# Gate columns of the last 512 tokens multiplied in another stage

## What is computed

```python
h = rms_norm(x, norm_w) * (1 + scale) + shift
proj = h @ w_in                                   # 2888 columns
u_pool, g_pool, q, k, v, g_attn, qi, ki, wi = split(proj)
pool_out = pool_mixer(u_pool, w_pool, pool_scale) * silu(g_pool)
q, k = rope(rms_norm(q)), rope(rms_norm(k)); qi, ki = rope(qi), rope(ki)
# for each block of 128 queries: index scores from qi, ki, wi; the 256 best keys; softmax attention over them
attn_out = dsa_attention(q, k, v, qi, ki, wi) * silu(g_attn)
x = x + gate * (concat(pool_out, attn_out) @ w_out)
```

## Time and profile before

| | us |
|---|---|
| median of 3 runs | 3118.52 (3115.85 to 3120.24) |
| the profiled execution | 3117.05 |
| its span, first to last instruction | 3115.3 |
| PE busy in the span | 2970.5 (95%) |
| DVE, ACT, POOL busy | 2233.0, 1620.9, 286.5 |
| mean granted TensorE clock | 0.98 |

### The profile page before, as it was taken

One profiled execution on the slowest core, in us unless ns is written; L12 is line 12 of the kernel. 1 busy time (PEld: TensorE's weight loads), 2 busy tenths in 40 slices (PEclk: granted clock), 3 DMA queues, 4 the chain that ended last, 5 costly groups with the idle time before them and its releaser, 6 DMA issues. The chain is left out here.

```text
span 3115.3 us, 48337 instructions
## 1 busy us (share of the span) xinstructions
PE 2970.5 (95%) x17496; PEld 2372.5 (76%) x17496; DVE 2233.0 (72%) x3265; ACT 1620.9 (52%) x2911; POOL 286.5 (9%) x673
## 2 busy tenths in 40 slices
PE   6999999999999999999999999999977899998899
PEld 5888888888878786777777888887756667776687
DVE  8888887766676758888879676324378989877553
ACT  5343422232455536777768433212278888887510
POOL 0000000000000001110100000000021432333100
PEclk8999999999999999999999999999979999998999
DMA  4434422257755333111126334322641111111774
GB/s 122 124 105 119 160 68 68 68 183 257 221 151 175 136 109 104 30 34 50 46 82 217 122 92 135 131 93 77 171 95 43 32 28 25 32 32 35 162 223 139
DMA packets 375234, 334.66 MB, mean 107 GB/s; under 512 B 97274, under 2 KB 328186, under 8 KB 368972
## 3 DMA queue, kind: packets, MB, share of 16 engines
q1 hardware_dynamic: 368676, 294.73, 33.1%
q0 software_dynamic: 5600, 36.51, 3.3%
q10 hardware_dynamic: 720, 0.31, 0.0%
HBM read 212.84 MB, written 108.68 MB: 103 GB/s over the span
## 5 line engine op out<-in xcount | busy, mean ns | idle before, releaser
L678 PE MATMUL p_oa_acc<-s_h_a_hi,s_mx_w_hi 128*128 128x512 f32 x744 | 291.4, 392 | 11.7 <-DVE s_h_a_lo L420 9.4
L325 ACT ACTIVATE s_mx_w_hi<-s_mx_raw 128x512 fp32r<-128x512 f32 x224 | 138.5, 628 | 310.0 <-PE p_oa_acc L678 237.9
L678 PE MATMUL p_oa_acc<-s_h_a_hi,s_mx_w_lo 128*128 128x512 f32 x744 | 290.1, 390 | 0.0
L678 PE MATMUL p_oa_acc<-s_h_a_lo,s_mx_w_hi 128*128 128x512 f32 x744 | 290.0, 390 | 0.0
L1773 DVE TENSOR_TENSOR_SCAN s_st_prod<-s_st_soft,s_st_prod 128x512 f32<-128x512 f32 x192 | 234.7, 1268 | 15.0 <-ACT s_st_soft L1699 15.0
L3480 PE MATMUL p_sa_turn<-s_ident,s_sa_arg 128*128 128x128 f32 x1088 | 168.4, 292 | 46.7 <-ACT s_sa_prob L3077 29.1
L1699 ACT ACTIVATE s_st_soft<-p_st_z 128x512 f32<-128x512 f32 (+3 forms) x320 | 153.6, 534 | 111.8 <-PE p_st_z L1826 111.3
L462 DVE TENSOR_TENSOR s_mx_w_lo<-s_mx_raw,s_mx_w_hi 128x512 fp32r<-128x512 f32 x224 | 153.2, 684 | 53.8 <-ACT s_mx_w_hi L325 52.4
L3480 PEld LDWEIGHTS p_sa_turn<-s_ident,s_sa_arg 128*128 128x128 f32 x1088 | 122.4, 146 | 85.1 <-issue 60.5
L3060 ACT ACTIVATE s_sa_arg<-s_sa_arg,s_sa_low_top 128x128 f32<-128x128 f32 (+15 forms) x128 | 155.2, 1214 | 58.8 <-DVE s_sa_low_top L3212 57.6
L2568 PE MATMUL p_pr_ps<-s_h_hi,s_pr_w_hi 128*128 128x512 f32 (+1 forms) x680 | 184.7, 392 | 0.7 <-DVE s_pr_w_lo L2435 0.4
(11 more groups left out here) (437 smaller groups left out, 7363.5 us busy)
## 6 DMA issues: line engine op xcount, KB each, us to landing
s_mx_raw<-in_w_in_a SPq DMA_DIRECT2D x128, 256.0 KB, 3.9
s_pb_ada<-in_w_ada SPq DMA_DIRECT2D x16, 768.0 KB, 7.0
s_pr_raw<-in_w_in SPq DMA_DIRECT2D x21, 512.0 KB, 5.7
s_pr_work<-s_pr_stage SPq DMA_DIRECT2D x38, 256.0 KB, 4.4
d_rot_hi<-s_pr_rot POOLq DMA_DIRECT2D x9, 1024.0 KB, 4.3
d_rot_lo<-s_pr_stage POOLq DMA_DIRECT2D x9, 1024.0 KB, 6.3
d_y_t<-s_mx_y SPq DMA_DIRECT2D x16, 512.0 KB, 5.7
s_oa_y_raw<-d_y_t SPq DMA_DIRECT2D x16, 512.0 KB, 6.8
```

What stands on the lines that cost most here:

```text
L678: ins = nc.tensor.matmul(bank, w[:, m, k, :], a[:, m, k, :], start=(k == 0 and n == 0), stop=(k == KH - 1 and n == 2))
```

## The change

The last 512 tokens' columns of the eight gate blocks are no longer multiplied in the rotation stage. There a gate block has 3 chunks in place of 4, its split weights are stored to DRAM (d_gate_w, 1 MB for each gate, from SP), and the sum of squares within a gate block goes to k = 6 in place of 4. Behind a norm block, ACT and DVE split the next weights ahead of the high and low parts. In the selection stage the activations' last quarter stays where it was; tiles are placed so that it isn't overwritten, and users of those columns wait. The first three blocks get the eight gates at the due times GATES_AT, each as four quarters of 6 matmuls ahead of four products, in a bank of its own turn; ACT copies the result and SP stores it. SP loads the weights of gates 0 and 1 among the first keys, those of gates 2 and 3 at the end of its part for block 0, 4 and 5 for block 1, 6 at the beginning and 7 at the end for block 2. Keys from 1024 on move to SP's part for block 3. The output stage applies Silu to the gates of the last four tiles.

```diff
+GATE_ROWS = [of + P * n for of in (ROW_GP, ROW_GA) for n in range(4)]
@@ rotation: stores and SP
-            return [(stage[:, b % 2], p_t[first:first + P, :])]
+            to = KEPT_FROM if first in gates else SEQ
+            return [(stage[:, b % 2, 0:to], p_t[first:first + P, 0:to])]
+        def chunks(b):
+            return NT - 1 if is_gate(b) else NT
+            def keep_weights(b):
+                sp.wait_ge(lo_done, b + 1)
+                for half, of in enumerate((w_hi, w_lo)):
+                    sp.dma_start(gate_w[gates.index(order[b][1]), half], of[b % 2][:].bitcast(F32).rearrange("p k n -> p (k n)")).then_inc(space.gate_kept, 16)
             for b in range(B):
                 if b and b + 2 < B:
                     load(b + 2)
+                if b + 1 < B and is_gate(b + 1):
+                    keep_weights(b + 1)
                 if b in turned_rows:
                     load_swapped(b)
...
+            sp.wait_ge(space.gate_kept, 32 * GATES)
@@ rotation: ACT (DVE has the same order with take_low)
-                if b - 2 in turned_rows:
+                late = b - 2 in norms_of
+                if b - 2 in turned_rows and not late:
                     take_high(b - 2)
                 if b:
                     leave(b - 1)
                 if b + 1 < B:
                     split(b + 1)
+                if late:
+                    take_high(b - 2)
@@ rotation: TensorE
-                    if k == KC // 2 and b - 1 in norms_of:
+                    if k == (KC - 2 if is_gate(b) else KC // 2) and b - 1 in norms_of:
-                        for t in range(NT - 1 if b == 0 else 0, NT):
+                        for t in range(NT - 1 if b == 0 else 0, chunks(b)):
@@ selection: order
+    GATES_AT = (0.2, 2.0, 3.8, 5.0, 6.4, 7.8, 9.2, 10.6)
+    QUARTERS = 4
+    gate_first = [min(n for n, (at, _) in enumerate(timed) if at >= gate_at) for gate_at in GATES_AT]
@@ selection: SP
+            def load_gate(i):
+                sp.wait_ge(space.gate_kept, 32 * (i + 1))
+                if i >= 2:
+                    sp.wait_ge(gate_multiplied, i - 1)
+                for half, to in enumerate((gate_w_hi[:, 2 * (i % 2):2 * (i % 2) + 2, 1024:1536], gate_w_lo[i % 2][:, :, 1024:1536])):
+                    sp.dma_start(to.bitcast(F32), gate_w[i, half].rearrange("p (s n) -> p s n", s=2)).then_inc(gate_w_in[i % 2], 16)
+            def store_gate(i):
+                sp.wait_ge(gate_left, i + 1)
+                sp.dma_start(p_t[GATE_ROWS[i]:GATE_ROWS[i] + P, KEPT], gate_rows[i % 2]).then_inc(gate_out[i % 2], 16)
             for piece in range(2):
                 load_keys(sp, space, "attend", piece, rot_hi, rot_lo)
+                load_gate(piece)
...
-                load_keys(sp, space, "attend", 2 + piece, rot_hi, rot_lo)
             for qb in blocks:
                 if qb:
                     bring_inverse(qb - 1)
+                if qb == 2:
+                    store_gate(4)
+                    load_gate(6)
+                if qb == 3:
+                    store_gate(6)
+                    store_gate(7)
+                    sp.wait_ge(gate_multiplied, GATES)
+                    for piece in range(2, 4):
+                        load_keys(sp, space, "attend", piece, rot_hi, rot_lo)
...
+                for i in {0: (0, 1), 1: (2, 3), 2: (5,)}.get(qb, ()):      # behind load_qi, load_q and load_values
+                    store_gate(i)
+                    load_gate(i + 2)
@@ selection: ACT
+            def leave_gate(i):
+                act.wait_ge(gate_multiplied, i + 1)
+                if i >= 2:
+                    act.wait_ge(gate_out[i % 2], 16 * (i // 2))
+                nc.scalar.activation(gate_rows[i % 2], bank_of_turn(("gate", i))[:], ACT.Copy).then_inc(gate_left, 1)
+                    begun = number[kind, qb, h, m] - QUARTERS
+                    if begun in gate_first:
+                        leave_gate(gate_first.index(begun))
@@ selection: TensorE
+            def multiply_gate(i, quarter):
+                if quarter == 0:
+                    bank_free(pe, ("gate", i))
+                    pe.wait_ge(gate_w_in[i % 2], 32 * (i // 2 + 1))
+                for k in range(2 * quarter, 2 * quarter + 2):
+                    strip, cols = k // 4, slice(1024 + k % 4 * P, 1024 + k % 4 * P + P)
+                    w_hi, w_lo = gate_w_hi[:, 2 * (i % 2) + strip, cols], gate_w_lo[i % 2][:, strip, cols]
+                    for m, (w, a) in enumerate(split_pass_list(w_hi, w_lo, xt_hi, xt_lo)):
+                        ins = nc.tensor.matmul(bank_of_turn(("gate", i))[:], w, a[:, k, KEPT], start=(k == 0 and m == 0), stop=(k == KC - 1 and m == 2))
+                for quarter in range(QUARTERS):
+                    if n - quarter in gate_first:
+                        multiply_gate(gate_first.index(n - quarter), quarter)
@@ output: ACT, and DVE's split waits for it
+                if t in closed:
+                    act.wait_ge(m_in[j], 48 * (t // DEEP))
+                    nc.scalar.activation(g_raw[:, j], g_raw[:, j], ACT.Silu).then_inc(opened, 1)
```

More of the change, by code:

```diff
@@ L2221, in phase_project_rotate @@
     order += [("turn", ROW_KI, TAIL, None)] + [("plain", ROW_GA + P * n, P, None) for n in range(2, 4)]
-    gates = [first + P * n for first in (ROW_GP, ROW_GA) for n in range(4)]
-    assert sum(c for _, _, c, _ in order) == D_PROJ
+    gates = [first for kind, first, _, _ in order if first in GATE_ROWS]
+    assert gates == GATE_ROWS and sum(c for _, _, c, _ in order) == D_PROJ
     B = len(order)
@@ L2275, in phase_project_rotate, with is_gate, kept_to @@
         block = ctx.enter_context(nc.Block())
+        def is_gate(b):
+            return order[b][1] in gates
+        def kept_to(b):
+            return sum(is_gate(c) for c in range(b + 1))
+        def chunks(b):
+            return NT - 1 if is_gate(b) else NT
         def q_scale(b):
@@ L2375, in leave @@
                     act.wait_ge(out_done[b % 2], 16 * outs_of[b - 2])
-                gate = order[b][1] in gates
-                nc.scalar.activation(stage[0:cols, b % 2], ps[b % 2][0:cols], ACT.Silu if gate else ACT.Copy).then_inc(left, 1)
+                wide_to = chunks(b) * 512
+                nc.scalar.activation(stage[0:cols, b % 2, 0:wide_to], ps[b % 2][0:cols, 0:wide_to], ACT.Silu if is_gate(b) else ACT.Copy).then_inc(left, 1)
                 if b in norms_of:
@@ L2697, in phase_select_attend @@
     number = {p: n for n, p in enumerate(products)}
+    gate_first = [min(n for n, (at, _) in enumerate(timed) if at >= gate_at) for gate_at in GATES_AT]
+    assert all(b - a > QUARTERS for a, b in zip(gate_first, gate_first[1:])) and len(gate_first) == GATES
+    banked = []
+    for n in range(len(products)):
+        banked += [("gate", gate_first.index(n))] if n in gate_first else []
+        banked += [("product", n)]
+    bank_turn = {of: n for n, of in enumerate(banked)}
     units = [(s, g) for s in range(SLOTS) for g in range(len(groups_of(s)))]
```

85 lines of the change are left out of this document (63 added, 22 removed).

## The result

| | before | after |
|---|---|---|
| median of 4 runs, us | 3119.38 | 3164.34 |
| lowest and highest, us | 3115.85, 3126.41 | 3161.53, 3169.20 |
| profiled execution (its span), us | 3117.05 (3115.3) | 3169.2 (3167.4) |

The ratio is 1.0139, its 95% interval 1.0127 to 1.0151: the change makes the kernel 43 to 45 us slower. The prediction said 3121 within 3096 to 3140. The time lies outside that range: slower had the largest of the three chances (0.39), but none of the cases was this slow.

A forecast was written before the change was run, and what follows sets the result against it. TensorE was taken to bound rotation, while no engine fills selection's first three blocks (some 28 us of TensorE holes). Rotation -26.5 and selection +28.5 us sum to +2.0, a median of about 3121 us, range 3096 to 3140.

The forecast's parts named there:

- Four gates behind the q blocks: Rotation stage: shorter gate blocks gain 12.6 us (0.6 to 15.4), limited by a loop outside TensorE.
- the loop: Rotation: norm block's leave, squares, sum, root to low rows' issue, landing; 41.0 us a turn, bounding the shortened gate pairs.
- the kept weights: Rotation: 1 MB of writes per gate ahead of the stores delays each turn by 0.7 us (0 to 3.7).
- The stores become the bound: Rotation rival, chance 0.17: kept and loaded weights precede rotated rows, 3.7 us in each of four turns; total 3133.
- Two gates among the pool blocks: Rotation stage: their chains have room, so they gain 2 x 5.44 = 10.9 us.
- The last two gates: End of rotation: TensorE ends 10.9 us earlier, but the stage ends on SP's prefetches; gain 3.0 us.
- Waits for weights: Selection: TensorE waits for late weights, +9.0 us at gate 4 (6 to 11), +5.5 at gate 7 (2 to 7).
- The coupling: Selection's first three blocks: gates mostly fit into holes, but quarters, banks and the fifth product's wait cost +12 us.
- The copies: Selection: eight copies of gates on ScalarE, 0.6 us each, cost +2 us (0 to 4.8).
- The clock: All stages: activity releases the throttle, busy stretches run at 1.00; half a us allowed for the added waits' effect.
- gates at half clock: Selection rival, chance 0.11: gates run at the first two blocks' half speed, 17 us more; total 3138.
- The output stage: Gets 4 Silu passes on little-used ScalarE, rows loaded three tiles ahead; costs nothing.

The follow-up runs named there:

- e14: e4 plus 12 filling matmuls, whose result nothing reads, ahead of the sum of squares in each gate behind a q block; ratio 1.0137 to the kernel before.
- e17: e4 with VectorE doing two of the four products ahead of the reciprocal, the others left out; ratio 1.0111 to the kernel before.
- e2: e1 without writing the gates' weights to DRAM and without the wait for them; ratio 0.9928 to the kernel before.
- e4: The changed kernel with the gates' weights kept one step later, issued behind the swapped halves; ratio 1.0116 to the kernel before.
- e11: Kernel before with only gates GA0 and GA1 moved, each in one piece, one product ahead of the two longest TensorE waits; ratio 0.9977 to the kernel before.
- e12: e11 with its two gates ahead of products 60 and 100, where TensorE has no wait within several products; ratio 1.0003 to the kernel before.
- e5: The changed kernel with loads of gates 4, 5 and 7 (and the gate stores ahead of them) before block 3's and 4's queries; ratio 1.0125 to kernel before.
- e3: The changed kernel with all four chunks of each gate computed again in rotation, selection still multiplying the gates; ratio 1.0184 to the kernel before.
- e10: Changed kernel, weights kept behind swapped halves, gate loads earlier, each gate in one piece one product ahead of a hole; ratio 1.0002 to kernel before.
- e13: e10 with each gate one product later, exactly ahead of the product at which TensorE waits for a bank; ratio 1.0090 to the kernel before.
- e7: e5 without ScalarE's copies of the gates out of their banks, other rows stored in their place; ratio 1.0075 to the kernel before.
- e1: The changed rotation stage alone, weights kept; in selection no gate is loaded, multiplied, copied or stored; ratio 0.9955 to the kernel before.
- e16: e10 with 48 filling matmuls in the sums of squares and the values 1 first in SP's queue; ratio 1.0009 to the kernel before.

## Why the prediction was wrong, step by step

- **Four gates behind the q blocks, 12.6 us: wrong.** The q part won 0.9 us (by the first pool block's leave); the four turns took 183.7 us for 182.4 before. Two terms of the loop failed. It was put together from the root to the issue of the low rows (24.7 us) as if the reciprocal hung on the root alone. The row that was not read is the reciprocal's own, which had waited for the root for 0.68 us only; that wait bounds the gain. The loop is 43.0, not 41.0 (e14, e17), 6.0 us in three turns. On top come the kept weights: 1.6 us a turn for the 0.7 taken, and 5.3 in the first turn, which the step left nearly out, 8.5 in all for 2.8. Without any kept weights (e2) the q part wins 9.4 us; with the weights moved behind the swapped halves (e4) 6.2, half of the forecast.
- **The stores become the bound (rival, 0.17): right for this stage, in part by luck.** It was tied to leaves over 43 us apart, and they were 44.6; it gave the q part 0.6 us, and it won 0.9. But its price of 3.7 us a turn was too high (1.6 measured), which made up for a loop that was 2.0 us too short. The weights had a head start of 3.0 us on the high rows, so less than 1.5 MB of kept and loaded weights (3.7 us at the 401 GB/s of the earlier trace rows) still stood ahead. The Trainium skill (DMA: Bandwidth & Descriptors, Queues, rings and completion order) has the engines take turns between queues; no run here can tell that from a queue that is served first, since by either the rows would be late by what is left of the weights.
- **Two gates among the pool blocks, 10.9 us: right.** e11 and e12, which move no others, have 10.8.
- **The last two gates, 3.0 us, the stage ending on SP: right in kind.** TensorE stands still for 11.8 us while SP issues (2.5 before); what is left of the stage's 13.5 us after the other terms is 1.7 (13.5 - 10.9 - 0.9 that the q part has won by the first pool block's leave).
- **Waits for weights, 9.0 and 5.5 us: right in size**, 11.1 and 6.3; 1.9 at gate 0 were not foreseen. But e5 shows that gate 4's hung on more than the queries: with these moved, it stood behind a store, and still waited 8.3 us.
- **The coupling, +12 us: the main miss.** This is the step that failed most. Beside the late weights the selection grew by 60.2 - 18.3 = 42 us (e3), for the 14 taken for the coupling and the copies together. The step compared sums (43.5 us of matmuls, 28 us of holes) and let 31.5 us of the matmuls go into the holes and into a better clock, so that 12 were left. Only 12 us went in (e3); the other 31.5 and the 10.6 us of waits for the copies are the 42. Ratios of busy time from later blocks (85 and 97%) can't say how much fits: holes are waits for a bank, and a gate needs one too. Where each gate stands one product ahead, 27 us go in (e10: 15.6 of idle time, 11.8 of clock), close to the 31.5 assumed; where it stands in the hole, none (e13). The 10.6 us for the copies belong to the same step: it named the fifth product's wait and gave it no price.
- **The copies, +2 us: probably too low.** e7 leaves 3 to 6 us for the eight copies themselves; no run shows them alone.
- **The clock.** Blocks 0 to 2 have 0.81, 0.85 and 0.91; from the same points they had 0.77, 0.74 and 0.91 before. The Trainium skill (TensorE: Matmul & The Clock Gate, Part 1) has activity release the throttle. e10's block 1, where TensorE is busy for 92%, agrees with 1.00; the change's block 1 is busy for 68%, less than the 74% before, and still has the higher clock, so the share of a whole block doesn't settle it. The rival of gates at half clock (17 us) fell: over the selection TensorE is busy 47.1 us longer than before in the kernel after and 44.5 in e3, for 43.5 at full clock. What half clock there is follows the late weights: behind the wait of 11.1 us gate 4's first 12 matmuls start 0.43 us apart and not 0.23. Half a us for this, as the sum had it, was too little; in the kernel after it is 3.6.
- **The output stage, nothing: right.** From the copy of block 4's outputs to the end it is 642.9 us before and 643.0 after.
- **The balance.** The rotation missed 12.5 us (14 for 26.5, e1) and the selection 28.5 (57 for 28.5, e3): 41 of the 43 us between 3121 and 3164.

## What to carry over

A hole in an engine's timeline can be filled only by work that doesn't need what the hole waits for: look up which buffer it is, and put the work before it, where it still has one of its own. When a loop across engines is summed up to find its new length, go through each engine's queue, too: the wait in front of the next instruction is the most that an earlier input can give. And move only the part whose gain lands on the path; here two of eight gates gave 10.8 us of rotation for 2.6 of selection, the other six some 9 more (e10) for 17 more (e16).

## What the runs showed of the hardware

- The sum's eight matmuls took 3.5 us (granted clock 0.57) after a wait of 2.50 us for the squares in the kernel after, 1.96 us after one of 1.19 in e17 and 1.87 with no wait in e14 (both 1.00); shortening a wait also gave the clock back.
- The same 1286 matmuls of the selection took 210.8 us of TensorE's busy time in e10 (granted clock 0.94) and 223.9 in e13 (0.90), where TensorE is idle for 52.0 us and not 39.3. So 12.7 us more of idle time came with 13.1 us of slower matmuls.
- 1 MB of writes issued 3.5 us ahead of the low rows (3.0 ahead of the high rows) on another queue delayed the landing of both by 1.6 us (7.9 for 6.3, and 5.9 for 4.3).
- A load of 256 KB (values 1) behind two gates' weights and the keys in the same queue took 10.5 us from issue to use in e11 and 12.8 in e12, which issue the same loads in the same order, where with a nearly empty queue it took 6.1.
